# One block for output projection, router, shared expert, routing and expert loop, with routing in two batches and 37 expert turns

## The reference, cut to what matters

```
x   = LayerNorm(alpha * x + h @ w_out)               # 544 x 1024
s   = sigmoid(x @ w_router)                          # 64 experts
sel = s + b_router
group score = sum of the two best sel of each group of 8 experts; keep the 4 best groups
idx = the 6 best experts of what is left; weights = s[idx] / sum * 2.5
routed = sum over the 6 experts e of weight * ((silu(x @ w_gate[e]) * (x @ w_up[e])) @ w_down[e])
shared = (silu(x @ ws_gate) * (x @ ws_up)) @ ws_down
x   = LayerNorm(alpha * x + routed + shared)
```

## Time and profile before

| | |
|---|---|
| time, median of 3 runs | 2313.07 us (2308.89 to 2314.68) |
| the profiled execution's own time | 2300.54 us |
| its span, first to last instruction | 2298.3 us |
| mean granted clock of PE | 0.901 |
| PE busy | 1894.2 us (82%) |
| DVE busy | 845.0 us (37%) |
| DMA over the span | 353.78 MB, mean 154 GB/s |
| first block of the three | 1417.6 to 1623.9 us |
| first `gate_up` of the expert loop | 1641.55 us |
| last down product | ends at 2201.2 us |

### The profile page before, as it was taken

How to read it: one execution, slowest core, us unless ns; L and a number is a source line. 1 busy time by engine, 2 the same in 40 slices (tenths; PEclk the granted TensorE clock), 3 DMA queues, 4 the chain that set the end, 5 groups by cost and what they waited for, 6 DMA issues and landing times. The chain is left out here.

```text
span 2298.3 us, 27505 instructions
## 1 busy us (share of the span) xinstructions
PE 1894.2 (82%) x10502; PEld 1285.4 (56%) x10502; DVE 845.0 (37%) x1954; ACT 573.2 (25%) x1298; POOL 327.0 (14%) x362
## 2 busy tenths in 40 slices
PE   7599999998998667999988888984799888898820
PEld 4277777777777566888766655351544334343300
DVE  0034345345345411016688552414322222222128
ACT  1121331331322301026567532210011111111111
POOL 0001001011011011003245260000111111111000
PEclk9799999999999858989899998987699999999965
DMA  2521211211110007305200366400699999999834
GB/s 102 175 66 29 57 49 29 54 39 42 48 32 9 21 0 172 87 17 180 77 2 1 111 214 222 178 3 0 247 378 415 420 419 407 415 394 405 348 134 158
DMA packets 159890, 353.78 MB, mean 154 GB/s; under 512 B 36680, under 2 KB 114032, under 8 KB 134384
## 3 DMA queue, kind: packets, MB, share of 16 engines
q1 hardware_dynamic: 139600, 291.71, 34.7%
q0 software_dynamic: 20160, 60.31, 7.4%
HBM read 333.45 MB, written 35.79 MB: 161 GB/s over the span
## 5 line engine op out<-in xcount | busy, mean ns | idle before, releaser
L718 PE MATMUL bank<-xT,arena 128*128 128x272 f32 x1280 | 325.9, 406 | 1.8 <-DMA arena<-in_w_in 1.2
L718 PEld LDWEIGHTS bank<-xT,arena 128*128 128x128 f32 x1280 | 243.1, 197 | 48.6 <-DMA arena<-in_w_in 1.4
L2529 PE MATMUL bank<-arena 128*64 128x512 f32 (+1 forms) x624 | 247.4, 639 | 25.5 <-issue 24.6
L2529 PEld LDWEIGHTS bank<-arena 128*64 128x64 f32 (+1 forms) x624 | 80.2, 156 | 135.1 <-issue 135.1
L1053 POOL TENSOR_TENSOR arena<-arena 128x512 f32<-128x512 f32 x48 | 52.3, 1090 | 634.3 <-DVE arena L1155 434.6
L2556 PE MATMUL bank<-arena 128*64 128x512 f32 (+1 forms) x408 | 131.8, 598 | 2.4 <-issue 1.9
L1389 PE MATMUL bank<-xT,arena 128*128 128x272 f32 x512 | 120.0, 398 | 13.1 <-DMA arena<-in_w_in 13.1
L2625 DVE SCALAR_TENSOR_TENSOR arena<-arena,bank 128x256 f32<-128x256 f32 x38 | 18.3, 480 | 276.9 <-ACT arena L2573 276.9
L1389 PEld LDWEIGHTS bank<-xT,arena 128*128 128x128 f32 x512 | 98.9, 193 | 34.0 <-DMA arena<-in_w_in 13.3
L2529 PE MATMUL bank<-hT,arena 128*64 128x512 f32 (+1 forms) x208 | 102.4, 650 | 12.4 <-issue 12.4
L2529 PE MATMUL bank<-xT,arena 128*64 128x512 f32 (+1 forms) x192 | 89.0, 618 | 9.6 <-issue 9.6
(11 more groups left out here) (507 smaller groups left out, 3322.5 us busy)
## 6 DMA issues: line engine op xcount, KB each, us to landing
arena<-in_w_exp_down SPq DMA_DIRECT2D x51, 1024.0 KB, 24.5
arena<-in_w_exp_gate SPq DMA_DIRECT2D x39, 1024.0 KB, 12.2
arena<-in_w_exp_up SPq DMA_DIRECT2D x39, 1024.0 KB, 26.6
arena<-in_w_in SPq DMA_DIRECT2D x48, 512.0 KB, 4.1
kvt<-in_w_exp_down SPq DMA_DIRECT2D x13, 1024.0 KB, 26.4
hT<-in_w_exp_gate SPq DMA_DIRECT2D x13, 1024.0 KB, 12.4
hT<-in_w_exp_up SPq DMA_DIRECT2D x13, 1024.0 KB, 26.7
xT<-in_w_exp_gate SPq DMA_DIRECT2D x12, 1024.0 KB, 11.6
```

Source lines behind the costliest of these rows:

```text
L718: last = mm(banks[2 * (i % 2) + half][:, 0:HALF], wh[blk % RING][:, k, :], xT[:, k, half * HALF:(half + 1) * HALF], start=(k == 0), stop=( ...
L2529: last = mm(banks[2 + 4 * (t % 2)][cols, :], xgT[:, k, cols], ewgu[i % EBUF][:, :, k], start=(k == 0), stop=(k == KD - 1))
```

## The change

The first and the second block become one, and the order of the work in it is written anew.

- PE takes the turning and the logits of a tile between the projections of later tiles, and the sample tile's two halves are put side by side in the array's columns (`project_sample`). The shared expert is computed turned (`shared_in`: its weights stand in the array, tokens move, in two parts of 256 and 288 tokens), so that its hidden rows need not be turned; its products stand between the logits, the counts and the first lists.
- DVE does the routing in two batches (`BATCHES`: tiles 0 to 2, then 3 and 4), with halving `max`/`min` steps for the 40 `max` and one `tensor_tensor_scan` for each row of doubling steps. `norm` has two wide instructions for three, ACT gives a square root, and DVE its reciprocal.
- SP waits for `s_up_banked` and for the new `order_saved` and then starts the load of the third expert; there is no barrier any more between the routing and the loads.
- `FIXED, HEAVY` are 2 and 10: 10 + 27 = 37 turns. The first five turns are experts 0 and 1 and three pairs.
- The gain and offset of the last normalisation are loaded in the last block, and waited for there.
- Tiles are laid out anew in the same memory; `slots` counts from 1.

```diff
-FIXED, HEAVY, LIGHT = 4, 12, 64
+FIXED, HEAVY, LIGHT = 2, 10, 64
-TURNS = [(0,), (1,), PAIRS[0], (2,), PAIRS[1], (3,), PAIRS[2]]
+TURNS = [(0,), (1,)] + PAIRS[0:3]
...
         @block.sync
-            early = [i for i in range(2, EBUF) if RANKS[i] < FIXED]
...
-            for i in range(2, NE):
+            sp.wait_ge(s_up_banked, 4)
+            sp.wait_ge(order_saved, 1)
+            for i in range(FIXED, NE):
...
         @block.tensor
+            project(0, 0)
+            project(0, 1)
+            project(1, 0)
+            project(1, 1)
+            turn_rows(0)
+            project(2, 0)
+            logits(0)
+            turn_rows(1)
+            project(2, 1)
+            logits(1)
+            project(3, 0)
+            turn_rows(2)
+            project(3, 1)
+            logits(2)
+            project_sample()
+            turn_rows(3)
+            pe.wait_ge(sh_in, 48)
+            shared_in(0, 0, 0)
+            logits(3)
+            shared_in(0, 0, 1)
+            turn_rows(4)
+            pe.wait_ge(res_ready, 10)
+            shared_in(0, 1, 0)
+            logits(4)
+            shared_in(0, 1, 1)
+            pe.wait_ge(x1t_ready, 2 * NTILE)
+            shared_in(1, 0, 0)
+            shared_in(1, 0, 1)
+            pe.wait_ge(mask_ready, len(BATCHES) + 1)
...
+            last.then_inc(cnt_banked, 1)
+            pe.wait_ge(s_sg_ready, 2)
+            pe.wait_ge(s_h_ready, 2)
+            shared_in(1, 1, 0)
+            shared_in(1, 1, 1)
+            make_list(0)
+            shared_down(0)
+            pe.wait_ge(s_sg_ready, 4)
+            shared_down(1)
+            pe.wait_ge(perm_ready, 2)
+            mm(banks[6][0:1, 384:448], rank64[0:NE, 2 * NE + 1:2 * NE + 2], rk[2][0:NE], start=True, stop=True)
+            mm(banks[6][:, 448:512], ones[0:NE, :], rk[3][0:NE], start=True, stop=True).then_inc(order_banked, 1)
+            make_list(1)
+            pe.wait_ge(s_h_ready, 4)
+            shared_down(2)
+            make_list(2)
+            shared_down(3)
+            shared_down(4)
+            pe.wait_ge(s_y_added, 2 * NTILE)
             turn(0)
...
         @block.vector
+            for t in range(4):
+                norm(t)
+            best_groups(0, 3, 1)
+            norm(4)
+            best_experts(0, 3)
+            best_groups(3, NTILE, 3)
+            best_experts(3, NTILE)
+            shared_products(0)
...
+            step(V.tensor_copy(order[0:1, :], banks[6][0:1, 384:448]), order_saved)
...
+            dve.wait_ge(x1_out, 16 * NTILE)
+            add_shared(0)
+            keep_list(1)
+            match(2)
+            add_shared(1)
+            add_shared(2)
+            keep_list(2)
+            add_shared(3)
+            add_shared(4)
...
         # last block
+            for n, name in enumerate(("ln2_g", "ln2_b")):
+                sp.dma_start(lnw[:, n], io[name].to_broadcast([P, D])).then_inc(w_in, 16)
```

569 lines of the change are left out of this document (295 added, 274 removed).

## The result

The changed kernel takes 2227.81 us in the median of 4 runs (2219.84 to 2232.5), the kernel before 2310.98 beside it (4 runs, 2305.09 to 2314.68): ratio 0.9639, 95% interval 0.9603 to 0.9675, 83 us less. The forecast was 2241 us, range 2222 to 2264. The profiled execution took 2232.50 us for a span of 2230.6; PE's mean granted clock is 0.906.

The account below looks back on a forecast made before the run. The expert loop was taken as bound by the weights' stream, idle until SP's first load. Terms -75 (earlier first load), 0 (turns), +3 (last block) gave -72 from 2313.07: 2241 us, own range 2232 to 2250, wider 2222 to 2264.

Parts of the forecast that it names:

- The step that carries it: Before the expert loop: first weight load 131 us after PE's first projection instead of 206.2, gain 75 us, between 60 and 81.
- Work in the block: New block, PE's first product to the list of experts: 125.7 us with waits, so first load at 127.4.
- cold groups: Rival: narrow product groups in the new block run at half clock, and the wide product behind pays too; 2252 us, chance 0.17.
- sample tile: New block: its projection takes 6.9 us with halves side by side; PE waits 3.6 us for its `norm` before turning it.
- the mask: New block: PE waits 0.5 us after `shared_in` for DVE's routing of batch two, which ends at 104.
- positions and counts: New block: 30 position and 20 count records on PE, warm, take 5.2 us.
- `shared_in` over 256 columns: New block: each such shared expert product takes 3.43 us on PE, half the columns in half the time.
- PE decides in the loop: Rival: PE, not the stream, sets the expert loop, so shift and saved turn both count; 2228 us, chance 0.06.
- the turns: Expert loop: one turn less and the new order change the time by 0, from -13 to +5 us.
- The last block: Two 0.5 MB loads now issued ahead of the `y_rows` rows cost +3 us, between 0 and 4.
- a late first turn: Rival at the loop's head: the first `gate_up` falls behind the loads; at 37 us 2251 us, chance 0.10.
- no gain: Rival: loads start earlier, but a slower or buffer-stopped stream loses as much; 2313 us, chance 0.03.

Follow-up runs that it names:

- one-batch: Changed kernel with routing of all five tiles in one batch (BATCHES has one entry), behind the last logits: 2237.92 us, ratio 0.9688.
- grouped: Changed kernel with PE's work in groups: all tiles projected, then all turned, then all logits, then the shared expert: 2238.98 us, ratio 0.9682.
- The changed kernel again: Changed kernel with no edit, run once more as a base: 2228.05 us, ratio 0.9646 to the kernel before.
- late loads: Changed kernel with SP waiting for DVE's last addition of the shared expert before the third expert's load: 2240.45 us, ratio 0.9694.
- four buffers: Changed kernel with four weight buffers in place of five: 2244.72 us, ratio 0.9708.
- first turn earlier: Changed kernel with the first turn's rows turned before the shared expert's last two down products, the last one behind the first `gate_up`: 2222.83 us, ratio 0.9614.
- earlier order: Changed kernel with the order of experts made ahead of the last `shared_in` and saved at once, so loads start earlier: 2224.76 us, ratio 0.9615.
- half `gate_up`: Changed kernel with `gate_up` multiplying only 4 of 8 slices of the hidden size, same weights loaded: 2218.69 us, ratio 0.9587.
- all three edits: Changed kernel with order of experts saved earlier, first turn's rows turned earlier, last norm's weights loaded behind the first y rows: 2223.05 us, ratio 0.962.

## Why the prediction was right, point by point

**The step that carries it held.** The first load behind the order was the end of the idle DMA time; it came 81.6 us earlier and the whole program 83. Work in the block: I computed 127.4 and took 131. Measured 124.6 and 123.3, just under my lower bound of 125. What I had added for cold groups (3.6) was not needed: all narrow groups up to there were warm, between wide products and with no wait over 2.1 us. Most of the rest is waits: 2.04 before the sample tile for 3.6, and none for the mask for 0.5. The remaining terms were close: sample tile 7.0 (1498.97 to 1505.96) for 6.9, positions and counts 5.2 for 5.2 (by my own 0.11 to 0.12 for each of 50 records the sum should have had 5.5 to 6), `shared_in` over 256 columns 3.5 for 3.43. So -75 was mis-sized; it is -82. This is 6.4 of the 11 us by which the gain of 72 was too small; the loop is the other 4.5. The measured 2227.8 thus lies below the forecast's own 2232 to 2250, inside the wider range only. It is also, by chance, the 2228 of the rival in which PE decides in the loop, whose mechanism the middle of the loop refutes.

**The clock.** I weighed the Trainium skill (TensorE: Matmul & The Clock Gate, Part 1: The HAM clock gate) against the row of narrow products at 0.53. By the rule that sustained activity releases the clock, nothing between the block's cold start and the list of experts would be cold, and so it was. But the one-batch and the grouped kernels show again what the row before showed, against that rule: PE busy without a pause for 13.6 us and granted 0.50.

What sets it off is shown for one batch: the same products behind the same wide ones run at 1.00 in the changed kernel, and the wait of 4.44 us is what differs ahead of them. The length of a wait alone does not tell. In the changed kernel 2.04 us before the sample tile left the clock at 1.00, while 1.58 us behind the list of experts stood beside half clock (5.15 us for eight records). In the grouped kernel the clock fell 2 us into the run. Whether 80 narrow records in a row would fall with no wait ahead of them no run here shows.

**The loop.** I took 0 for the turns, out of -13 to +5. Measured -4.5 from first load to last down, and -2.6 and -3.7 in the two other profiles of the same loop; with the old turns it is +1.0. The size is near the scatter of one loop, and the turn and the order were not taken apart. In the middle the stream is the bound: five single turns from 1759.65 to 2008.81 make four rounds of 62.3 us for 62.8 before, and halving `gate_up` gave 10.5 of 127 us. So PE's work pays only at the loop's head and end.

**The last block.** +3 expected, between 0 and 4; +3.2 measured, and moving the loads takes it away. In four later profiles it is about 5 (29.0 to 29.5 us for 24.2), so that the close hit is in part luck.

**What failed is a reason, not the number**: "A change before the stream counts one for one if it brings the first load forward." Loads 19.4 us later moved the last down by 10.4, loads 11.9 us earlier moved it by 6.1 and, in the second profile of that loop, 3.3: about half or less, both ways. It held for the change only since the first load and the first `gate_up` moved together (by 81.6 and 81.2), so that the loop started in the same state. The prediction had the piece for it, the buffers freed by the first `gate_up` 27 us behind the first load (measured 27.06), but drew only one side: it priced a later `gate_up` and missed that moving the loads by themselves counts for half. In its place stands: the end moves with the transfers done by the time the buffers stop being the limit. The changed kernel again is the base; its own two profiles differ by 1.4 in the first column.

| kernel against the changed one again | transfers in the head | last down |
|---|---|---|
| late loads | -9.0 | +10.4 |
| four buffers | -8.4 | +8.6 |
| one batch | -7.2 | +9.2 |
| grouped | -8.0 | +12.1 |
| first turn earlier | +0.2 | -1.8 |
| earlier order | +3.8 to +5.2 | -5.5 to -6.1 (-3.3 in its second profile) |
| half `gate_up` | +7.8 | -10.4 |
| all three edits | +4.2 to +5.6 | +1.1 |

Seven of eight have the right sign, six lie within 3 us. The last does not fit; the slow turns at its end stand above.

**The rivals.** Cold groups, PE deciding in the loop (it does at its head and end, not between), a late first turn and no gain did not happen here; the first was brought about by two edits.

## What to carry to other kernels

Where a stream of weights bounds a loop, ask when its buffers are all given away and what frees the first: an earlier load is worth only what can be moved before that, and the loads and the users that free the ring (here the first `gate_up` and the first down product) have to come forward together. Put narrow products between wide ones and keep PE from waiting ahead of them: a wait of 4.4 us cost 10, and grouping the same products cost 8.5 us of clock. Before pricing a loop's turns, find the parts that the stream does not bound, its head and its end; only there a shorter turn counts.

## What the runs showed of the hardware that was not expected

- Behind a wait of 4.44 us PE ran 13.6 us without a pause at half clock (0.50): 8.7 us of narrow products and 4.9 us of products with 288 columns.
- `tensor_tensor_scan` takes 0.42, 0.56 and 0.82 us for 128, 192 and 320 elements a partition, `tensor_tensor` 0.29, 0.36 and 0.49: about twice as much for each element, with the same start.
- Sixteen records of 32 rows in two column halves take 3.6 us, as long as eight records of 128 rows: the halves run fully side by side.
- The first `gate_up` took 8.79 us in one execution and 7.12 in another of the same loop, the clock over the 20 us around it was 0.92 and 1.00. Both came behind the same short waits.
